# When GpSimd splits weights beside VectorE: seven tiles of a banded-attention layer held back, and five small reorderings

## The reference

```python
def sliding_window_sink_attention(u, positions, w_qkv, sinks, w_o):
    ...
    q = rotary(q.reshape(B, S, SW_HEADS, SW_HD), positions).reshape(B, S, SW_KV_HEADS, SW_GROUP, SW_HD)
    ...
        s = jnp.einsum('blkgd,bckd->bkglc', qb, kb).astype(jnp.float32) * scale
        s = jnp.where(valid, s, -jnp.inf)
        m = jnp.maximum(jnp.max(s, axis=-1), sink)
        p = jnp.exp(s - m[..., None])
        den = jnp.sum(p, axis=-1) + jnp.exp(sink - m)
        ob = jnp.einsum('bkglc,bckd->blkgd', p, vb.astype(jnp.float32))
        ob = ob / jnp.moveaxis(den, -1, 1)[..., None]
    ...
    return out @ w_o
```

## Time and profile before

| what | value |
|---|---|
| median of three runs | 2425.8 us (2425.69 to 2426.35) |
| the profiled execution | 2426.36 us, span 2424.6 us |
| PE busy | 2361.2 us, 97% of the span |
| DVE, ACT, POOL busy | 1188.4, 1110.2, 1022.3 us |
| mean granted TensorE clock | 0.993 of full |

### The profile page before, as it was taken

The page is one execution under the profiler, slowest core; times in us unless marked ns, Lnnn a source line. Parts: engine busy times, 40 slices in busy tenths (PEclk is TensorE's granted clock), DMA queues, the critical chain, the costliest instruction groups (busy, mean ns, idle before and its releaser), DMA issues.

```text
span 2424.6 us, 40467 instructions
## 1 busy us (share of the span) xinstructions
PE 2361.2 (97%) x13258; PEld 1940.0 (80%) x13258; DVE 1188.4 (49%) x2342; ACT 1110.2 (46%) x2408; POOL 1022.3 (42%) x750
## 2 busy tenths in 40 slices
PE   7999999999999989999999999999889999999998
PEld 6878878778877768778888888888757888888886
DVE  5555555554667766854354322225585424422224
ACT  5344334434655556645555433234565645433232
POOL 4444444433433324433833544444212733544442
PEclk9999999999999999999999999999999999999999
DMA  5433333332322222222522323332222522333322
GB/s 188 116 96 99 94 104 105 101 100 94 116 88 87 89 64 83 78 70 96 165 62 75 111 94 98 93 95 83 87 66 71 152 82 69 109 93 96 96 94 78
DMA packets 126385, 232.52 MB, mean 96 GB/s; under 512 B 17184, under 2 KB 17312, under 8 KB 126240
## 3 DMA queue, kind: packets, MB, share of 16 engines
q1 hardware_dynamic: 123392, 220.08, 30.1%
q10 hardware_dynamic: 2848, 10.49, 1.2%
HBM read 208.48 MB, written 2.10 MB: 87 GB/s over the span
## 4 chain that ended last, share of the span: by engine, by line
issue 55%; POOL 23%; PE 21%; POOLq 1%; DVE 0%; DMA 0%; ACT 0%; DVEq 0%; ACTq 0%; SPq 0%
POOL wl L429 21%; PE PS L452 20%; POOL w L429 2%; PE PS L531 0%; PE PS L519 0%; POOLq L428 0%; PE PS L486 0%; POOLq L437 0%; DMA raw<-tiles_dram 0%; PE PS L526 0%; DVE work L2461 0%; DVE H L1911 0%; DVE ul L1901 0%; ACT work L1716 0%; POOLq L432 0%
## 5 line engine op out<-in xcount | busy, mean ns | idle before, releaser
L429 POOL TENSOR_TENSOR wl<-raw,wh 128x512 fp32r<-128x512 f32 x714 | 971.3, 1383 | 1306.6 <-ACT wh L1163 1305.2
L452 PE MATMUL PS<-uh,wh 128*128 128x512 f32 (+1 forms) x2056 | 758.3, 369 | 7.4 <-ACT work L1331 4.5
L452 PE MATMUL PS<-uh,wl 128*128 128x512 f32 (+1 forms) x2056 | 742.4, 361 | 0.0
L452 PE MATMUL PS<-ul,wh 128*128 128x512 f32 (+1 forms) x2056 | 741.9, 361 | 0.0
L1163 ACT ACTIVATE wh<-raw 128x512 fp32r<-128x512 f32 x714 | 411.9, 623 | 346.9 <-PE PS L452 277.9
L452 PEld LDWEIGHTS PS<-uh,wh 128*128 128x128 f32 x2056 | 390.1, 190 | 86.8 <-issue 14.2
L452 PEld LDWEIGHTS PS<-uh,wl 128*128 128x128 f32 x2056 | 389.9, 190 | 59.9
L452 PEld LDWEIGHTS PS<-ul,wh 128*128 128x128 f32 x2056 | 390.4, 190 | 55.1 <-issue 0.5
L452 PE MATMUL PS<-wh,hid_sb 128*128 128x512 f32 x1024 | 322.0, 396 | 0.0
L1331 ACT ACTIVATE work<-PS 128x512 f32<-128x512 f32 (+1 forms) x152 | 87.1, 573 | 328.7 <-PE PS L452 260.3
L452 PEld LDWEIGHTS PS<-wh,hid_sb 128*128 128x128 f32 x1024 | 192.5, 188 | 46.1
(11 more groups left out here) (245 smaller groups left out, 2701.6 us busy)
## 6 DMA issues: line engine op xcount, KB each, us to landing
raw<-tiles_dram SPq DMA_DIRECT2D x746, 256.0 KB, 2.7
work<-work SPq DMA_DIRECT2D x296, 64.0 KB, 2.0
gB<-post_dram ACTq DMA_DIRECT2D x8, 512.0 KB, 3.8
H<-x_dram SPq DMA_DIRECT2D x4, 512.0 KB, 6.3
H<-x_dram ACTq DMA_DIRECT2D x4, 512.0 KB, 4.9
work<-mem_dram ACTq DMA_DIRECT2D x2, 1024.0 KB, 6.5
out_dram<-H ACTq DMA_DIRECT2D x4, 512.0 KB, 2.6
cst<-consts_dram SPq DMA_DIRECT2D x1, 644.0 KB, 5.1
```

The source lines that it names most:

```text
L429: nc.gpsimd.tensor_tensor(w_of(wl, slot)[:, hc], raw[:, s, hc], w_of(wh, slot)[:, hc].bitcast(F32), ALU.subtract).then_inc(lo_ready, 1)
L452: last = nc.tensor.matmul(out, a, b, start=start and m == 0, stop=stop and m == 2)
```

## The change

Six edits. (1) In the banded layer POOL's subtraction for weight tiles sw+9+t, t = 0 to 6, waits in addition for `probs_ready`, until the weights of unit 4t+3 are scaled; for this POOL's loop over all tiles is cut in two, with 9 instead of 1 tiles written out. (2) In the differential layer's end ACT splits the fourth output-projection tile later, and (3) DVE makes `ul` of row 5 before the last steps of the norm instead of after unit 7's last weights; PE's piece (0,3,6) moves ahead of the last head's transposes. (4) At the end of ff0 the fourth row block is added, squared and brought to H before the third is normed. (5) In the two projections into the memory layers ACT splits the third following tile ahead of the last `square`. (6) In sw DVE makes `ul` of head 5 after unit 27, not 26.

```diff
-            def rest(n, slot, s):
+            def rest(n, slot, s, weights=None):
                 for h in range(2):
                     hc = slice(512 * h, 512 * h + 512)
                     pool.wait_ge(hi_ready, n * 2 + (h + 1))
+                    if weights is not None and h == 0:
+                        pool.wait_ge(probs_ready, weights)
...
+            if on("sw"):
+                in_units = BASE["sw"] + 9
+                rests(N_D, in_units)
+                for t in range(7):
+                    n = in_units + t
+                    rest(n, slot_of(n), n % 2, weights=UNIT["sw"] + 4 * t + 4)
+                rests(in_units + 7, n_tiles)
...
-                begin(n, u0, DIFF_EARLY[24:31])
+                begin(n, u0, DIFF_EARLY[24:32])
                 diff_outputs(7)
-                begin(n, u0, DIFF_EARLY[31:38])
+                begin(n, u0, DIFF_EARLY[32:38])
...
+                if mem_of is not None:
+                    split_g(b + 2)
                 square(order[3])
-                split_g(b + 2)
                 if mem_of is None:
+                    split_g(b + 2)
...
                 split_g(b + 2)
+                square(3)
                 split_g(b + 3)
-                norm_squares(H, [2])
-                square(3)
-                norm_squares(H, [3])
+                norm_squares(H, [2, 3])
...
-                split_g(b + 3)
                 diff_exps(7, 1, 0)
                 diff_pt(6, 3)
                 split_input(3, 4)
+                split_g(b + 3)
...
                 half_lo(gain, 0)
+                added(3)
                 times_gain(2)
                 bring(2, at + 5)
-                added(3)
                 times_gain(3)
-                norm_row(H, 2, at + 6)
-                bring(3, at + 7)
+                bring(3, at + 6)
+                norm_row(H, 2, at + 7)
                 norm_row(H, 3, at + 8)
...
                     diff_max(7, 3)
+                    split_lo(5, 6)
 
                 diff_norm(6, 0, between=weights_2_max_3)
                 diff_weights(7, 1, 3)
-                split_lo(5, 6)
...
-                    heads = {21: (0, 1), 22: (1, 2), 23: (2, 4), 24: (4, 5), 26: (5, 6), 30: (6, 7)}.get(k)
+                    heads = {21: (0, 1), 22: (1, 2), 23: (2, 4), 24: (4, 5), 27: (5, 6), 30: (6, 7)}.get(k)
```

More of the change, by code:

```diff
@@ L434, in _, with rests @@
                     rest(i * D_TILES + j, j % D_RING, j % 2)
[L435 to L441, removed]
+            def rests(first, end):
+                turns = (end - first) // G_RING
+                if turns:
+                    with pool.Fori(0, turns) as i:
+                        for j in range(G_RING):
+                            rest(i * G_RING + (first + j), slot_of(first + j), (first + j) % 2)
+                for n in range(first + turns * G_RING, end):
+                    rest(n, slot_of(n), n % 2)
+            if on("sw"):
[5 more added lines that the diff above has]
+                rests(in_units + 7, n_tiles)
+            else:
+                rests(N_D, n_tiles)
         @block.tensor
```

## The result

| | before | changed |
|---|---|---|
| median | 2426.07 us (2425.69 to 2428.72, 4 runs) | 2412.68 us (2411.03 to 2417.44, 4 runs) |
| profiled execution | 2426.36 us, span 2424.6 | 2411.03 us, span 2409.2 |
| ratio | | 0.9943, 95% interval 0.9931 to 0.9956 |

The direction was right and 2412.68 us is just inside the range, at its lower end. The gain of 13.4 us (by the interval 11 to 17) is twice the forecast 6.8. The number is almost that of the first rival (2412.8 us, "the swaps are in time"), and the traces show that this rival is false. So the agreement is luck, and the parts have to be looked at one by one.

What follows compares the result with a forecast made beforehand. PE is busy for 97% of the span, so only its waits and half-clock stretches can be won. Gains of 0.6 + 4.3 + 1.4 + 0.5 = 6.8 us bring the median from 2425.8 to 2419.0 us, range 2412.5 to 2425.5.

Steps and rivals of the forecast that it cites:

- first rival: Banded layer: swapped tiles arrive in time, gaining 6.8 us there instead of 0.6, 13.0 in all, 2412.8 us; chance 17%.
- Edit 1, POOL and DVE exclude each other: Banded layer: they block each other instruction by instruction; held subtractions meet unit 4t+4's small sum and scaling, 0.9 us lost.
- Edit 1, SP's queue: Banded layer: swap DMAs stand behind the held loads, DVE waits 0.6 to 1.4 us a turn; five turns lose 3.0 us.
- D: Banded layer: time from the fourth swap DMA's issue to its landing, mean 2.75 us; a turn takes 11.4 + D.
- Edit 6: Banded layer, head 5: 2.0 us gained for sure and 1.0 more if the clock holds; 3.0 taken.
- Edits 2 and 3: End of the differential layer: 0.85, 2.0 and 1.4 us gained, sum 4.3, bounds 2.0 and 4.6.
- without the idle time ahead I take that back too: End of the differential layer: 1.4 us lost to clock 0.64 in window 884 to 888 is regained.
- The 0.4 us that "stays": End of the differential layer: unit 7's last weights, transposed one piece later, still leave 0.4 us of wait.
- Edit 4: End of ff0: 1.5 us of block 2's norm comes behind H's update, under ACT's sum; gain 1.4, bounds 0.5 and 2.0.
- Edit 5: Memory layers x0 and x1: the evacuation's split comes out about 0.3 us earlier, twice; 0.5 gained, bounds 0 and 2.8.
- Slower rival: Banded layer: PE's clock halves in each turn after waits of 1.8 us, 2431.2 us; chance 6%.

Runs made afterwards that it cites:

- swaps first: Changed kernel with the four swap DMAs of query tiles 6 to 11 ahead of the weight load in SP's queue: 2412.47 us; repeated, 2410.57 us.
- without the hold: Changed kernel without edit 1 and with the swap DMAs ahead of the loads: 2415.03 us against 2428.26 before, ratio 0.9944.
- the kernel with the split behind the table: On top of swaps first, ACT loads its table ahead of the fifth output-projection tile's split at the differential layer's end: 2409.26 us against 2428.26, ratio 0.9920.
- the two profiles: The changed kernel profiled in its first run (2412.68 us) and when run once more as the mark on one chip (2414.56 us, ratio 0.9947).
- the early adding: Kernel before with half of edit 4, DVE adding the fourth row block ahead of the third's gain: 2426.60 us against 2426.63, ratio 0.9995.

## Why the prediction was right in sign and wrong in size

**Edit 1, POOL and DVE exclude each other:** right. No scaling of units 6, 10, 14 or 18 is over 0.7 us now, and the small one of unit 4t+4 is the new victim (up to 1.16 us in place of 0.48).

**Edit 1, SP's queue:** right in place and mechanism: the fourth swap 4.7 us after POOL's start (4.8 forecast), DVE idle 1.1 to 1.5 us before it in five turns (0.6 to 2.5 forecast) and 0.3 in the sixth, released by the swap DMA. The size was off: "So in five turns the change loses 5 x 0.6 = 3.0 us" rested on D = 2.75, the mean of before. D came out at 2.0 to 2.2 in them, so five turns lost nothing (13.55 against 13.56). From the first product with the values to the 22nd it is 71.92 us before (1815.04 less 1743.12) and 71.58 in the change (1803.08 less 1731.50). Why D was up to 3.8 us before is not settled; where a hold delays the loads it was never over 2.6 (three executions, fourth DMA of each turn). With the swaps ahead of the loads it was 2.0 in every turn of swaps first, both times, but 2.8 in one turn without the hold, and 2.5 and 3.3 in two turns of the kernel with the split behind the table.

**Edit 6:** right, 3.6 us alone against 3.0, since the half clock behind it was gone too. In the whole change the banded layer gained 3.25.

**Edits 2 and 3:** 4.5 us in the two profiles against 4.3, but this agreement flatters. Of the 65.93 us of before, 1.6 were a half clock that three of the five executions with neither edit 2 nor 3 show, and two don't; the windows of two of them (same columns), the kernel with edit 1 alone and the one with the early adding:

```profile
884.00:888.00 4.00, 4.00 (x23) 3.37 (x22) 1.44 (x4) 1.64 (x3) 1.79 (x2) 1.00 0.20 68
```

```profile
884.00:888.00 4.00, 4.00 (x14) 3.23 (x13) 1.47 (x4) 1.63 (x3) 1.52 (x2) 0.58 0.23 68
```

PE waits 2.43 us ahead of it in both. So the sure gain is 2.9 us, or 1.7 where the tie is lost, and the term "without the idle time ahead I take that back too" counted as certain what happens in only some of the executions. The 0.4 us that "stays" was 0.23 or 1.42 us, by the tie.

**Edit 4:** here is the step that failed most: "Gain 1.4". The part gained 4.6. On the chain, the last transposes come 2.4 us earlier, not 1.4: I took off the third block's norm and left out the two operations of `added`, which edit 4 moves too and which are worth 0.7 us alone. The other 2.2 us are the clock, whose half stretch behind the 4.35 us wait I had read in no row, although I counted such a stretch in two other places. All seven executions without the whole of edit 4 have a half-clock stretch there, of 3.4 or 6.8 us, and the seven with it have none. Part of that is chance too: among the executions with the old end the half stretch was 6.8 us in three, where the part took 60.9 to 61.1 us, and 3.4 in two, where it took 59.8. Against those two the gain is 3.4 us. The waits themselves came out as foreseen, one of 1.19 us ahead of block 2 and one of 0.59 ahead of block 3.

**Edit 5:** 1.2 us against 0.5. PE's first wait in x0 fell from 1.73 us to 0.82:

```profile
1155.84 0.39 PE L466 MATMUL PS<-uh,wh 128*128 128x256 f32 x1 [0.82 <-ACT work L1346]
```

It was not run alone. In the x0 column, rows of equal half clock can be compared: 357.9 to 358.3 us without it and 357.0 to 357.2 with it at 3.4 us of half clock, 359.6 to 360.0 and 358.8 to 358.9 at 6.8. That is 0.9 and 1.0 us for x0. The 0.45 us from the banded layer's end to behind x1 is no more than equal code differs by: this stretch took 201.4 to 202.4 us in the seven executions without edit 5 and 200.7 to 201.7 in the seven with it. The half clock itself comes and goes with no regard to edit 5.

**The sum.** Forecast 0.6 + 4.3 + 1.4 + 0.5 = 6.8; by the two profiles 3.25 + 4.5 + 4.6 + 1.2 = 13.5. The misses are ff0's end (3.2), the banded layer (2.7) and the memory layers (0.7), all one way. The first rival named the right time for a wrong cause: it gained its 6.2 us more in the banded layer, where 2.7 came.

**Slower rival:** the clock did not halve in each turn. PE's waits of 0.9 to 1.3 us there left it at 2.4 GHz. It was at 1.2 GHz behind unit 21, where PE waited 1.79 us, over 10.2 us in the first profile of the change and over 3.4 in the second, which had another stretch of 3.4 at the layer's start.

## What to carry to other kernels

Before holding an instruction back on one engine, list what stands in program order behind everything that it releases: the hold was worth some 4 us, and all of it was lost to four small DMAs that stood behind a load in one queue. When PE waits long, look up the granted clock behind that wait as well, each time: half of the largest gain here was clock. And read gains of a microsecond from the same part in several executions, since a tie between two engines or a half-clock stretch that is not always there can move one profile by 1.2 to 1.7 us.

## What the runs showed of the hardware that was not expected

Two instructions of DVE and POOL recorded as starting within 10 ns of each other can go either way, at 0.16 us or 1.30 us for a four-element operation. The record shows POOL first in all seven traces, though DVE got through in four of them, so at this scale it does not tell which issued first. The Trainium skill, "SBUF — State Buffer", section "Who interferes with whom", says that whoever issues first has the shared ports for the whole instruction; the rows agree in that the one that is held off waits for the other's whole instruction (1.30 us, where POOL's took 1.29), and add that with static programs the order can differ from one execution to the next.

The half clock behind one and the same wait of 2.43 us came in three executions and not in two others. By the trace it is no fixed price of a wait of that length. And ahead of 855 us executions of programs that are equal there differ by up to 4.7 us (853.3 to 857.9). The granted clock goes with it: the two with no half clock there are the fastest (853.3 and 853.5), the nine with a stretch near 20 us alone come to 855.0 to 856.3, and the three with another of 3.4 us near 621 us to 857.5 to 857.9.
